# Seven products for the second contraction half of key and query blocks in neighbourhood attention, with weight sums made by transfers

## What is computed

```python
q, k, v = jnp.split(h @ w_qkv, 3, axis=-1)      # h: 256 x 2048, w_qkv: 2048 x 6144, 16 heads of 128
q = rms_norm(q.reshape(shp), q_gain)            # per head
k = rms_norm(k.reshape(shp), k_gain)
s = einsum(q, k_window) * scale + bias          # window of 16 columns by the rows there are
p = softmax(s)
out = einsum(p, v_window).reshape(B, T, D_MODEL)
return out @ w_o
x = x + that
```

## Time and profile before

| | |
|---|---|
| median of 3 runs | 2090.65 us |
| profiled execution, its own time | 2090.62 us |
| its span in the trace | 2088.8 us |
| TensorE clock granted | 1.00 throughout the work |
| busy, share of the span | TensorE 100%, VectorE 75%, ScalarE 55%, GpSimd 2% |
| one head group (1132.0 to 1206.6 us) | 74.6 us |
| DMA engines in that stretch | share 0.50, 180 GB/s |

### The profile page before, as it was taken

How to read it: one execution, slowest core, us unless ns; L and a number is a source line. 1 busy time by engine, 2 the same in 40 slices (tenths; PEclk the granted TensorE clock), 3 DMA queues, 4 the chain that set the end, 5 groups by cost and what they waited for, 6 DMA issues and landing times.

```text
span 2088.8 us, 27472 instructions
## 1 busy us (share of the span) xinstructions
PE 2082.3 (100%) x10850; PEld 1765.4 (85%) x10850; DVE 1559.8 (75%) x2067; ACT 1144.0 (55%) x1425; POOL 51.6 (2%) x44
## 2 busy tenths in 40 slices
PE   9999999999999999999999999999999999999999
PEld 8888888888888888888788888888888888888887
DVE  7798787878778877678775566556779688688775
ACT  6777565565564565665555545454545545454452
POOL 0000000000000000000010011000000000000000
PEclk9999999999999999999999999999999999999999
DMA  8565555555654744346564544456676666666664
GB/s 325 194 240 194 195 209 194 199 212 182 210 192 142 254 163 153 143 171 212 201 214 174 187 176 166 163 180 218 190 229 209 202 224 199 222 188 195 242 181 141
DMA packets 67424, 411.81 MB, mean 197 GB/s; under 512 B 7392, under 2 KB 14304, under 8 KB 19808
## 3 DMA queue, kind: packets, MB, share of 16 engines
q1 hardware_dynamic: 64992, 393.28, 52.4%
q0 software_dynamic: 2304, 16.78, 4.4%
HBM read 407.80 MB, written 2.23 MB: 196 GB/s over the span
## 4 chain that ended last, share of the span: by engine, by line
PE 98%; DVE 1%; ACT 1%; issue 0%; POOL 0%; DVEq 0%
PE bank L1146 26%; PE bank L1168 15%; PE bank L1170 15%; PE bank L1172 15%; PE bank L1151 14%; PE bank L1184 2%; PE bank L1186 2%; PE bank L1188 2%; PE bank L1267 1%; PE bank L1403 1%; PE bank L1339 1%; PE bank L1391 0%; PE bank L1361 0%; PE bank L1297 0%; PE bank L1372 0%; PE bank L1416 0%
## 5 line engine op out<-in xcount | busy, mean ns | idle before, releaser
L1894 DVE TENSOR_TENSOR wlo<-raw,whi 128x2048 fp32r<-128x2048 f32 x314 | 718.4, 2289 | 216.1 <-ACT whi L1463 185.1
L1463 ACT ACTIVATE whi<-raw 128x2048 fp32r<-128x2048 f32 x314 | 600.3, 1912 | 254.5 <-PE bank L1172 234.6
L1146 PE MATMUL bank<-A,whi 128*128 128x512 f32 x2448 | 586.7, 392 | 0.0
L1146 PEld LDWEIGHTS bank<-A,whi 128*128 128x128 f32 x2448 | 451.3, 188 | 90.3 <-issue 1.3
L1151 PEld LDWEIGHTS bank<-A,wlo 128*128 128x128 f32 x2432 | 311.8, 191 | 11.8
L1151 PE MATMUL bank<-A,wlo 128*128 128x256 f32 x2432 | 315.4, 283 | 0.0
L1168 PE MATMUL bank<-whi,A2h 128*128 128x512 f32 x768 | 301.1, 392 | 0.0
L1170 PE MATMUL bank<-whi,A2l 128*128 128x512 f32 x768 | 299.2, 390 | 0.0
L1172 PE MATMUL bank<-wlo,A2h 128*128 128x512 f32 x768 | 299.0, 389 | 0.0
L1168 PE MATMUL bank<-whi,A 128*128 128x512 f32 x608 | 241.4, 397 | 0.0
L1172 PE MATMUL bank<-wlo,A 128*128 128x512 f32 x608 | 237.4, 390 | 0.0
(11 more groups left out here) (267 smaller groups left out, 1893.3 us busy)
## 6 DMA issues: line engine op xcount, KB each, us to landing
raw<-wst SPq DMA_DIRECT2D x308, 1024.0 KB, 4.8
W<-wst SPq DMA_DIRECT2D x37, 1024.0 KB, 4.9
W<-wst POOLq DMA_DIRECT2D x10, 1024.0 KB, 8.3
W<-cum_scratch SPq DMA_DIRECT2D x8, 1024.0 KB, 7.0
raw<-wst POOLq DMA_DIRECT2D x6, 1024.0 KB, 8.0
W<-rows SPq DMA_DIRECT2D x21, 256.0 KB, 6.1
W<-first SPq DMA_DIRECT2D x12, 384.0 KB, 7.2
W<-exp_scratch SPq DMA_DIRECT2D x16, 256.0 KB, 6.4
```

The costliest lines, as they stand in the source:

```text
L1146: last = e.matmul(o[:, :], whi[:, s, k * P:(k + 1) * P], A1[:, k, :, :].rearrange("p h t -> p (h t)"), start=k == 0, stop=packed and k == ...
L1463: e.activation(whi[:, u % 3, :], raw_of(u), ACT.Copy).then_inc(*hi.inc((u, 3)))
L1894: e.tensor_tensor(wlo[:, u % 3, :], raw_of(u), whi[:, u % 3, :], ALU.subtract).then_inc(*lo.inc((u, 3)))
```

## The change

For head groups 1, 2 and 3 the key and query products share a Strassen seven over the second half of the contraction (tiles 8 to 15). The activations there are the 2 x 2 blocks of (token block) by (contraction tiles 8 to 11, 12 to 15), the weights the 2 x 2 blocks of (tiles 8 to 11, 12 to 15) by (query columns, key columns). Tiles 0 to 7 of key and query and all of value stay "B" units. A group thus has 8 "B" units and 7 "P" units, where it had 12 "B" units, in this order (K key, Q query, V value; positions 0 to 14):

```diff
+HEADS_SEVEN = (1, 2, 3)
+MIX_HEADS = -2
...
+    for j in HEADS_SEVEN:
+        u += in_turn("--a-c-b-e-d-f-g", sevens("np", "na_w_qkv_2", j, 0, "acbedfg"),
+                     heads("nk", j)[:2] + heads("nq", j)[:2] + heads("nv", j))
+    no = [b(("no", nb), "na_w_o_2", nb * 512) for nb in range(ND)]
+    u += no[0][:3] + no[1][:3] + no[0][3:] + no[1][3:] + no[2] + no[3]
...
-        k0, q0 = at["nk", j, 3] + 1, at["nq", j, 3] + 1
         if j == 0:
-            k0 += 1
+            k0 = at["nk", 0, 3] + 2
             after[k0].append(("r2", 7))
-        run(("nk", j), k0, 3)
+            run(("nk", 0), k0, 3)
+            run(("na", 0), at["nq", 0, 3] + 1, 9)
+            after[at["nv", 0, 3] + 5].append(("mix", MIX_HEADS))
+            continue
+        last = at["np", j, 0, "g"]
+        run(("nk", j), last - 1, 3)
         if j < KVH - 1:
-            run(("na", j), q0, 9)
+            run(("na", j), last + 1, 9)
         else:
...
+            after[no[0]] += [("na", j, 0), ("na", j, 1)]
+            for i, n in ((1, 2), (2, 4), (3, 6), (4, 8)):
+                mid[no[i]].append(("na", j, n))
+                if n < 8:
+                    after[no[i]].append(("na", j, n + 1))
...
+    if u + 2 < len(units) and units[u + 2][1][0] == "np":
+        then = {"a": "b", "c": "f", "b": "d", "d": "g"}.get(name(u + 2))
+        if then:
+            yield ("acc", unit(u + 2, then))
+        return
...
+                seven_of = tag[0] in ("nk", "nq") and tag[1] in HEADS_SEVEN
+                owner = ((at["np", tag[1], 0, "c"], t) if seven_of and tag[0] == "nk" else
+                         (at["np", tag[1], 0, "eg"[t]], 0) if seven_of else (u, t) if form == "A" or tag[0] == "ao" else
...
+                if tag == ("np", HEADS_SEVEN[-1], 0, "g"):
+                    for t, last in enumerate((u, product(u, "f"))):
+                        w.wait_ge(*hi((last, 3)))
+                        w.wait_ge(*lo((last, 3)))
+                        e.dma_start(XR[:, t, :], xr_scratch[t]).then_inc(s_back[t], 16)
...
+                if n == 5:
+                    for t in range(NT):
+                        w.wait_ge(*aff_v(("a", t, ND - 1), 1))
+                        e.dma_start(xr_scratch[t], XR[:, t, :]).then_inc(s_spill[t], 16)
...
+            def heads_drained(u, n):
+                _, j, _, name = units[u][1]
+                made = {x: at["np", j, 0, x] for x in "abcdefg"}
+                to, ps = drains(units[u][1])[n], bank[BANK[u, 0]][:, :]
+                x = (nk if to[0] == "k" else nq)[:, int(to[1]), :]
...
+                if n and name != "b":
+                    w.wait_ge(*evac_v((u, 0)))
+                    e.tensor_tensor(x, x, nq[:, 1, :], ALU.subtract).then_inc(*evac_v.inc((u, n)))
+                else:
+                    w.wait_ge(*mm_done(u))
+                    e.tensor_tensor(x, ps, x, ALU.add).then_inc(*evac_v.inc((u, n)))
...
-                w.wait_ge(*evac_a((at[kind, j, 3], 1)))
+                w.wait_ge(*(evac_v((at["np", j, 0, "f"], 1) if kind == "nk" else (at["np", j, 0, "g"], 0))
+                            if j in HEADS_SEVEN else evac_a((at[kind, j, 3], 1))))
```

More of the change, by code:

```diff
@@ L442, in stack_kernel @@
         RAW, READY, FREED = {}, {}, {}
[L443 removed]
+        loads, accs, holder = [0] * (RING + 4), [0] * (RING + 4), [None] * (RING + 4)
         def product(u, name):
@@ L450, in last_read @@
             name = units[u][1][3] if units[u][0] == "P" else None
+            if units[u][1][0] == "np" and name == "e":
+                return u
             return {"a": lambda: product(u, "g"), "c": lambda: product(u, "f"),
@@ L509, in evac_order @@
                     key = s[1:]
+                elif s[0] == "late" and units[s[1]][1][0] == "np" and units[s[1]][1][3] in ("a", "c"):
+                    if on_act:
+                        yield from ((s[1], t) for t in range(NT))
+                    continue
                 elif s[0] == "late" and units[s[1]][0] == "P":
@@ L521, in stack_kernel, with empties @@
         evac_a, evac_v = Marks(sem("emptied_a"), evac_order(True)), Marks(sem("emptied_v"), evac_order(False))
+        def empties(key):
+            tag = units[key[0]][1]
+            return evac_a if tag[0] in ON_ACT or tag[0] == "np" and tag[3] in ("a", "c") else evac_v
         def emptied(marks, key):
@@ L739, in side_uses @@
                 yield ("upb", r[0]), r[0]
+            elif what == "mm" and units[r[0]][1][0] == "np" and units[r[0]][1][3] in "abdf":
+                yield ("np", units[r[0]][1][1], units[r[0]][1][3]), None
             elif what == "mm" and units[r[0]][1][0] == "bp" and units[r[0]][1][3] in "abdf":
@@ L752, in stack_kernel @@
             BEFORE[bp[x], 0] = None, SIDE["bp", x][1]
+            for j in HEADS_SEVEN:
+                u = at["np", j, 0, x]
+                BANK[u, 0] = 4 + SIDE["np", j, x][0]
+                BEFORE[u, 0] = None, SIDE["np", j, x][1]
         def side_free(use):
@@ L764, in stack_kernel @@
             u = s[1] if len(s) > 1 else None
-            if s[0] in ("evac", "late") and units[u][1][0] in ("bo", "bp"):
+            if s[0] in ("evac", "late") and units[u][1][0] in ("bo", "bp", "np"):
                 continue
@@ L897, in norm_w, with tmp_of @@
             return CO[:, c:c + 1]
-        def tmp_of(r):
+        def tmp_of(r, c=0):
+            if r == 1 and c > 1:
+                return [W[:, N_KT + (2 * c - 4 + i) * 512:N_KT + (2 * c - 3 + i) * 512] for i in range(2)]
             base = M_TMP if r == 2 else N_PT if r == 1 else W_S + 2048
@@ L992, in load @@
                         w.wait_ge(*lo((split, 3)))
-                        if name == "e":
+                        if name == "e" and units[before][1][0] != "np":
                             w.wait_ge(*add_v(product(before, "g")))
@@ L1160, in token_block @@
                 opens = tag[0] == "ao" or tag[-1] == 0
+                alone = tag[0] == "nk" and tag[1] in HEADS_SEVEN and tag[2] == 1
                 for k in ks:
@@ L1171, in token_block @@
                     w.wait_ge(*lo((u, piece)))
-                    last = e.matmul(o, h, wl, start=False, stop=t in shut(tag) and k == 3)
+                    last = e.matmul(o, h, wl, start=False, stop=(t in shut(tag) or alone and t == 1) and k == 3)
                 if 3 in ks:
```

156 lines of the change are left out of this document (106 added, 50 removed).

## The result

| | before | after |
|---|---|---|
| median | 2091.29 us (4 runs, 2090.61 to 2092.54) | 2104.77 us (4 runs, 2103.79 to 2106.92) |
| ratio | | 1.0067, 95% interval 1.0055 to 1.008 |
| profiled execution, span | 2090.62, 2088.8 us | 2103.79, 2102.0 us |

The change makes the kernel 13 us slower. The forecast was 2098.5 us, in a range of 2086.0 to 2106.0. The span is 13.2 us longer. The timeline of TensorE says where: a landmark ahead of the neighbourhood attention (the transposes behind 1002 us) is 0.1 us later than before, and the first unit of the MLP behind it starts at 1432.69 us where it was 1419.46, which is 13.2 again. Nothing else of the program moved.

The account below looks back on a forecast made before the run. The prediction took packed TensorE as the bound, each matmul saved or new wait counting in full: -8.2 + 11.7 + 2.4 + 1.5 + 0.6 = +8.0 us, forecast 2098.5 us, 8-in-10 range 2086.0 to 2106.0.

Parts of the forecast that it names:

- rival 4: TensorE's clock falls to 1.2 GHz behind each of four waits, 2.7 us each: +11, 2109 us; chance 0.06.
- Fewer matmuls, -8.2: Key and query products on TensorE: 288 matmuls become 276 per group, 36 fewer at 0.227 us, saving 8.2 us.
- Three waits for g's drain, +11.7: Behind each group, position 15's second token block waits 3.8 us plus 0.1 for VectorE to drain g's PSUM bank.
- The clock behind a wait: TensorE's matmuls after a wait: the forecast's sum had no clock term; a lower clock was only rival 4.
- The query wait of group 3, +2.4: Middle of the second "no" unit: TensorE waits 2.4 us for normalised queries, 4.4 by the longer power.
- The keys of group 0, +1.5: Activation sums shift VectorE's low parts 3.4 us, so key transposes wait 1.5 us, 2.8 with the longer power.
- The queries of group 0, +0.6: Position 2 is now a "P" unit, so TensorE arrives 2.72 us sooner and waits 0.6 us for queries.
- Powers: GpSimd's power takes 1.64 us, or 3.61 beside a VectorE low part; the shorter taken for groups 0 and 3.
- Transfers at nothing: Summing transfers, the residual's store and its loads stay hidden, adding 0 us; landings take 8.0 us, 12.3 at most.
- rival 3: Late transfers: landings of 15 us make g's high part 1.5 us late in three groups, +4.5, 2103; chance 0.08.
- Rivals 1 and 2: Waits at group ends: first, lower prices, 2094 down to 2086, chance 0.22; second, no TensorE wait, 2082.5, chance 0.14.

Follow-up runs that it names:

- experiment 6: Kernel after with the edits of Experiment 1 and Experiment 4, and group 3's query steps one unit later in "no"; 2086.64 us, ratio 0.998 to the kernel before.
- Experiment 1: Kernel after with key normalisation and key transposes of groups 1 to 3 one step later, so g's drain precedes the stand for the power; 2094.85 us.
- experiment 3: Kernel after with GpSimd raising one column of eight to the power in the key steps of groups 1 to 3; 2099.63 us.
- experiment 2: Kernel after with the 12 summing transfers made plain overwriting transfers, the addition left out; 2103.33 us.
- experiment 5: Kernel after with seven unused matmuls of constants ahead of position 15's second token block in three groups, while TensorE waits for g's drain; 2100.49 us.
- experiment 8: experiment 7 with the scores of groups 0 to 2, and all behind them, a further step later; 2095.16 us.
- Experiment 4: Kernel after with the activation sums made five units earlier, behind the last value unit of group 0; 2101.39 us.
- experiment 7: experiment 6 with the query steps of groups 0, 1 and 2 beginning one step later; 2090.86 us, ratio 1.0001 to the kernel before.

## Why the prediction was right, and where its sum was off

The number lies inside the range of 2086.0 to 2106.0, and outside the forecast's own range of 2094 to 2102. The places of the waits were foreseen; that the total stayed inside is partly luck, as the range was meant to leave out rival 4, and rival 4's mechanism is what the forecast lacked.

- **Fewer matmuls, -8.2.** Right: 36 fewer; what is left after experiment 6, with its remaining waits counted, bears out the size to within 0.6 us.
- **Three waits for g's drain, +11.7.** Right in place, line and length: 10.7. Experiment 1 takes them away by moving two steps, experiment 3 shortens them by what it takes from the power, experiment 2 shows that the transfers have no part in them.
- **The clock behind a wait.** This is the step that failed: rival 4, given 0.06, is what happens, in all three groups. It costs +6.8 us in place of the nothing that the forecast had for it, and experiment 5 shows the cause apart from the wait, and the size within 1 us. The sign that the prediction had named for rival 4, a granted clock under 1.00, is there. Rival 4's own price, 2.7 us for one "P" unit's worth, was right (1.6, 2.6, 2.6), but not its count: three waits and not four. Behind it the Trainium skill (TensorE: Matmul & The Clock Gate, HAM oscillation) warns that gaps in TensorE's work lower its clock; the rows agree, 0.70 to 0.84 behind gaps of 3.6 us. In the rows of experiments 1, 3 and 8 the clock also fell behind some shorter waits, of 1.7 to 2.5 us. I set the warning aside because the kernel before had no wait over 1.3 us to test it by. Absence of a row was taken as evidence, and it was none.
- **The query wait of group 3, +2.4.** It measured 0. The wait's cause was right, as experiments 1, 3 and 5 bring it back with 3.4, 1.9 and 2.0 us; it was hidden because the slow matmuls ahead of it (2.6 us) gave VectorE the time. Two of the errors of the sum thus belong together: where the clock is paid, this wait is not.
- **The keys of group 0, +1.5.** +2.0, because the power took 3.62 us and not 1.64. The prediction had 2.8 for that case; the shift of the low parts was 2.5 us (1070.34 for 1067.83) and not 3.4. Experiment 4 removes the whole.
- **The queries of group 0, +0.6.** 0.6.
- **Powers.** 3.6 and 1.65 us, as the walk took them except for group 0's keys. The Trainium skill (GPSIMD Engine Reference, Specifications) says that GpSimd shares its SBUF interfaces with VectorE and contends with instructions of two SBUF inputs. The rows agree for every power that began inside a low part. But the prediction read them too simply when it set 1.64 against 3.61 as without and with a low part: its 1.64 ran beside one, having begun 0.04 us ahead of it, and experiment 7 repeats that. What the rows show is that a power begun inside a low part ends behind that part's end, by 0.43 us with one column (experiment 3) and 1.5 with eight.
- **Transfers at nothing.** Right: experiment 2, against rival 3. Between the first two long waits the DMA share is 0.71, where 0.8 was reckoned. That only one of 16 landings was far out could not be read from a median.
- **Rivals 1 and 2.** Neither the lower prices (at most 2.3 us a wait) nor the drain in time: the gaps are 3.58 us, and the 0.1 us pieces that could overlap shortened the chain by nothing that shows.

The sum by the measured terms: -8.2 + 10.7 + 6.8 + 0 + 2.0 + 0.6 + 0.7 = 12.6. The forecast of +8.0 was low by the clock, less the query wait that the clock hid. The range held the result through its upper end, which left room for late transfers and not for the clock.

## What to carry to other kernels

Shortening one engine's work by 8 us cost 13, 10 of it because one 0.7 us drain stood behind a wait of the same in-order engine: walk the order of the instructions for each new dependence, and place drains that free a PSUM bank ahead of any wait for a third engine. Price a wait of TensorE of some microseconds with the slow matmuls that may follow it, and where a wait can't be removed, try filler matmuls: here they gave back 4.3 us. Look also at which of two engines begins first where one holds the other up: 0.2 us in the start of a low part went with 2 us in the length of a power. When a step is moved later to be out of one wait, look up which buffer its reading frees, for the next writer may be an engine that everything else stands behind.

## What the runs showed of the hardware

- Behind gaps of 3.6 us on TensorE matmuls ran slow in all of nine cases in three profiled executions (kernel after, experiments 2 and 4), which cost 1.6 to 2.8 us each. Behind gaps of 2.5 us they did so in one of three (experiment 3). With matmuls of constants in gaps of 3.6 us they did so in none of three (experiment 5). Shorter gaps gave both: two waits in a row of 1.2 or 1.3 and 0.5 us before transposes had slow matmuls behind them in experiment 1 (group 0, waits of 1.27 and 0.54) and experiment 3 (group 3, 1.19 and 0.54), and none in experiment 5 (group 0, 1.19 and 0.54, and group 3, 1.23 and 0.54); behind three of 1.94 us no slow matmul followed (experiment 7); behind the first of three of 1.8 us the clock was 0.86 over 12 us, behind the other two it stayed 1.00 (experiment 8). The length of the gap alone does not decide it.
- A power of 128x8 on GpSimd that began 0.15 to 0.2 us behind the start of a VectorE low part took 3.6 us and ended 1.5 us behind the low part's end; one of 128x1 took 2.55 and ended 0.43 behind it. Without a low part beside it the power of 128x8 took 1.65, and it took 1.64 to 1.66 as well where it began 0.04 to 0.11 us ahead of a low part (group 0: kernel before, experiments 7 and 8). These low parts took 2.29 to 2.31 us, as ever.
- A 1 MB transfer that adds to SBUF landed in 8.2 us and kept the queue's share of all DMA time at 7.6%; the same 12 as plain copies landed in 5.2 us and the share was 6.0%, that is 1.6% of 2102 us over 12, 2.8 us less each at full share.
- Matmuls of 512 columns whose activations lie in `mixr` started 0.233 us apart, those from the other activation buffers 0.227 in the median and at most 0.230 (means of 12 matmuls, kernels before and after). What sets it was not tested.
